# Two mixer layers: the second attention's projections placed beside the first attention's steps, groups started at fixed steps

## The reference, cut to what matters

```python
proj = x @ w_in + b_in
(qa, ka, va, beta_raw, a_raw, za, qb, kb, vb, qc, kc, vc) = jnp.split(proj, split_at, axis=-1)
o_a = gated_deltanet(qa, ka, va, beta_raw, a_raw, za, ...)   # convolution, gates, delta rule by chunks
o_b = chunk_relpos_attention(qb, kb, vb, rel_bias)           # 4 heads of 128
o_c = swa_sink_attention(qc, kc, vc, sinks)                  # 8 heads of 64, 2 of keys and values
gates = jax.nn.sigmoid(x @ w_gate + b_gate).reshape(b, t, 3, d)
merged = (gates[:, :, 0] * (o_a @ w_br_a) + gates[:, :, 1] * (o_b @ w_br_b)
          + gates[:, :, 2] * (o_c @ w_br_c))
return merged @ w_out
```

## Time and profile before

| | |
|---|---|
| median of 3 runs | 2259.19 us (2258.14 to 2260.42) |
| span of the profiled execution | 2258.2 us |
| instructions in it | 34613 |
| TensorE busy | 2223.4 us, 98% |
| VectorE busy | 1630.9 us, 72% |
| ScalarE busy | 1198.2 us, 53% |
| POOL busy | 129.2 us, 6% |
| read from HBM | 403.98 MB, mean 180 GB/s |

### The profile page before, as it was taken

One profiled execution on the slowest core, in us unless ns is written; L12 is line 12 of the kernel. 1 busy time (PEld: TensorE's weight loads), 2 busy tenths in 40 slices (PEclk: granted clock), 3 DMA queues, 4 the chain that ended last, 5 costly groups with the idle time before them and its releaser, 6 DMA issues.

```text
span 2258.2 us, 34613 instructions
## 1 busy us (share of the span) xinstructions
PE 2223.4 (98%) x14127; PEld 1903.4 (84%) x14127; DVE 1630.9 (72%) x2508; ACT 1198.2 (53%) x1896; POOL 129.2 (6%) x185
## 2 busy tenths in 40 slices
PE   8999999999999999999999999999999999989999
PEld 7888899878888888888898777888878888867887
DVE  5777768867676876768668867776877678666776
ACT  5555446644555545555356444555454655546553
POOL 2100010120000000000100110000000000420000
PEclk9999999999999999999999999999999999999999
DMA  7755574445555556656554446555655655643654
GB/s 242 226 190 188 186 226 122 141 140 187 189 186 194 188 185 210 191 188 198 194 180 141 141 136 211 189 187 174 205 173 176 207 187 188 197 128 118 197 178 149
DMA packets 284207, 408.17 MB, mean 181 GB/s; under 512 B 13828, under 2 KB 171072, under 8 KB 283792
## 3 DMA queue, kind: packets, MB, share of 16 engines
q1 hardware_dynamic: 276096, 380.84, 52.6%
q0 software_dynamic: 7808, 25.04, 3.8%
q10 hardware_dynamic: 144, 0.07, 0.0%
HBM read 403.98 MB, written 1.91 MB: 180 GB/s over the span
## 4 chain that ended last, share of the span: by engine, by line
PE 89%; DVE 6%; ACT 3%; DMA 1%; issue 1%; POOL 0%; SPq 0%; DVEq 0%; ACTq 0%
PE PS L569 24%; PE PS L475 12%; PE PS L477 12%; PE PS L476 12%; PE PS L568 11%; PE PS L472 2%; PE PS L473 2%; PE PS L474 2%; PE PS L571 2%; DVE WL L1385 2%; PE PS L552 1%; PE PS L551 1%; PE PS L550 1%; PE PS L492 1%; DVE QX L1692 1%
## 5 line engine op out<-in xcount | busy, mean ns | idle before, releaser
L1385 DVE TENSOR_TENSOR WL<-RW,WH 128x1024 fp32r<-128x1024 f32 (+2 forms) x678 | 805.6, 1222 | 168.6 <-ACT WH L1001 164.5
L569 PE MATMUL PS<-XT,WH 128*128 128x512 f32 x2368 | 807.9, 394 | 0.0
L1001 ACT ACTIVATE WH<-RW 128x1024 fp32r<-128x1024 f32 (+2 forms) x678 | 680.9, 1042 | 210.9 <-PE PS L477 44.1
L568 PE MATMUL PS<-XT,WL 128*128 128x256 f32 x2072 | 580.7, 280 | 0.0
L569 PEld LDWEIGHTS PS<-XT,WH 128*128 128x128 f32 x2368 | 425.2, 188 | 76.0
L568 PEld LDWEIGHTS PS<-XT,WL 128*128 128x128 f32 x2072 | 389.8, 188 | 13.4
L475 PE MATMUL PS<-WH,XT 128*128 128x512 f32 (+3 forms) x624 | 241.5, 387 | 1.5 <-issue 0.7
L477 PE MATMUL PS<-WH,XT 128*128 128x512 f32 (+3 forms) x624 | 233.4, 374 | 0.0
L476 PE MATMUL PS<-WL,XT 128*128 128x512 f32 (+3 forms) x624 | 233.2, 374 | 0.0
L475 PE MATMUL PS<-WH,HTH 128*128 128x512 f32 x488 | 192.4, 394 | 0.0
L477 PE MATMUL PS<-WH,HTL 128*128 128x512 f32 x488 | 191.7, 393 | 0.0
(11 more groups left out here) (513 smaller groups left out, 3256.2 us busy)
## 6 DMA issues: line engine op xcount, KB each, us to landing
RW<-in_w_ff_in SPq DMA_DIRECT2D x252, 512.0 KB, 4.3
RW<-in_w_ff_out SPq DMA_DIRECT2D x128, 512.0 KB, 4.4
RW<-in_w_in SPq DMA_DIRECT2D x56, 512.0 KB, 4.5
RW<-in_w_gate SPq DMA_DIRECT2D x48, 512.0 KB, 4.2
RW<-in_ffn_gate SPq DMA_DIRECT2D x44, 512.0 KB, 4.4
RW<-in_ffn_up SPq DMA_DIRECT2D x44, 512.0 KB, 4.7
RW<-in_ffn_down SPq DMA_DIRECT2D x44, 512.0 KB, 4.5
RW<-in_w_out SPq DMA_DIRECT2D x16, 512.0 KB, 5.0
```

The source lines that it names most:

```text
L568: self.e.matmul(k.PS[:, b.n, 0:T], wl, k.XTH[:, kt, :], start=False, stop=False)
L569: ins = self.e.matmul(k.PS[:, b.n, :], wh, k.XT[:, kt, :], start=kt == 0, stop=kt == 7)
L1001: self.e.activation(u.hi_out, raw, ACT.Copy).then_inc(*self.s["hi"].up(u.n))
L1385: self.e.tensor_tensor(u.lo_out, raw, u.hi_out.bitcast(F), ALU.subtract).then_inc(*self.s["lo"].up(u.n))
```

## The change

The projections of attention c become the generator `inputs_c`, the first part of `inputs_a`: 8 half steps for the queries, 4 steps for keys and values. The swap of the keys is done behind the first half step of the first of delta's projections. The filler then has 44 steps. The nine groups start at the steps 0, 4, 8, 14, 18, 22, 26, 30 and 34 in place of 0, 3, 6 ... 24, so that `attend` has 44 steps too.

```diff
         while gens or live:
-            if gens and n % 3 == 0:
-                live.append(gens.pop(0))
+            while gens and n >= gens[0][0]:
+                live.append(gens.pop(0)[1])
...
-        bks = [self.bank() for _ in range(4)]
-        run(self.cols(w_in, 3592, 4, bks, self.x))
-        for j in range(4):
-            e.query_c(l, j, bks[j])
-            self.drop(bks[j], ("proj_v", (l, "qc", j)))
-        kb, vbs = self.bank(), [self.bank(), self.bank()]
-        for k0 in range(0, 8, KU):
-            u = self.take(wsrc(w_in, k0, KU, 4104, 256))
-            e.kv_part(u, k0, kb, vbs, self.x)
-            self.free(u)
-        e.kv_out(l, kb, vbs)
...
-        b = self.bank()
-        e.kv_swap(l, b)
-        self.drop(b, ("proj_v", (l, "kc2")))
...
+        def inputs_c():
+            bks = [self.bank() for _ in range(4)]
+            yield from self.cols(w_in, 3592, 4, bks, self.x, steps=2)
+            for j in range(4):
+                e.query_c(l, j, bks[j])
+                self.drop(bks[j], ("proj_v", (l, "qc", j)))
+            kb, vbs = self.bank(), [self.bank(), self.bank()]
+            for k0 in range(0, 8, KU):
+                u = self.take(wsrc(w_in, k0, KU, 4104, 256))
+                e.kv_part(u, k0, kb, vbs, self.x)
+                self.free(u)
+                if k0 == 6:
+                    e.kv_out(l, kb, vbs)
+                    self.drop(kb, ("proj_v", (l, "kc")))
+                    for t in range(2):
+                        self.drop(vbs[t], ("proj_v", (l, "vc", t)))
+                yield
+
+        def swapped():
+            b = self.bank()
+            e.kv_swap(l, b)
+            self.drop(b, ("proj_v", (l, "kc2")))
+
         def inputs_a():
+            yield from inputs_c()
             for part in (0, 1, None, 2):
...
                 bks = [self.bank() for _ in range(4)]
-                yield from self.cols(w_in, 512 * part, 4, bks, self.x, steps=2)
+                yield from ending(self.cols(w_in, 512 * part, 4, bks, self.x, steps=2), 0 if part == 0 else None, swapped)
...
-        self.attend(gens, fill)
+        self.attend(list(zip((0, 4, 8, 14, 18, 22, 26, 30, 34), gens)), fill)
```

More of the change, by code:

```diff
@@ L2934, in mixer1 @@
                 self.drop(bks[j], ("proj_v", (l, "qk", 4 * part + j)))
-        bks = [self.bank() for _ in range(4)]
-        run(self.cols(w_in, 3592, 4, bks, self.x))
-        for j in range(4):
-            e.query_c(l, j, bks[j])
-            self.drop(bks[j], ("proj_v", (l, "qc", j)))
-        kb, vbs = self.bank(), [self.bank(), self.bank()]
-        for k0 in range(0, 8, KU):
-            u = self.take(wsrc(w_in, k0, KU, 4104, 256))
-            e.kv_part(u, k0, kb, vbs, self.x)
-            self.free(u)
-        e.kv_out(l, kb, vbs)
-        self.drop(kb, ("proj_v", (l, "kc")))
-        for t in range(2):
-            self.drop(vbs[t], ("proj_v", (l, "vc", t)))
-        b = self.bank()
-        e.kv_swap(l, b)
-        self.drop(b, ("proj_v", (l, "kc2")))
         todo = []
```

## The result

The changed kernel takes 2280.82 us, the median of four runs (2279.79 to 2286.09). The kernel before, in four runs beside it, takes 2258.66 us (2256.7 to 2260.42). The ratio is 1.0101, with an interval of 1.0084 to 1.0118: slower by 22.2 us. The forecast was 2258.4 us, with a range of 2253 to 2264, so the result lies outside it, on the side that had a chance of 0.14. The profiled execution of the changed kernel took 2286.09 us, the longest of the four, with a span of 2284.3 us.

What follows compares the result with a forecast made beforehand. TensorE, with work 98% of the span and 89% of the chain, was taken to bound the kernel. Terms -4.2 + 1.9 + 0.2 + 3.2 + 1.7 - 3.6 = -0.8 us off 2259.2 gave about 2258.4 us, range 2253 to 2264.

Steps and rivals of the forecast that it cites:

- the side that had a chance of 0.14: Whole kernel: slower by over 0.2%, chance 0.14.
- Part 1: Attention stretch, both layers: three TensorE waits for PSUM banks and small ones beside them go, -4.2 us.
- the waits only move within the attention stretch: Rival, attention stretch: other bank pairs come close, half the bank gain, -2.1 us; total 2260.5 us; chance 0.2.
- Part 2: First group's scores in the first attention: they come too early for their key and query sums, +1.9 us.
- Part 3: Attention stretch: possible new waits, mainly a tight bank for the second projection's fourth column, +0.2 us.
- Part 4: Ahead of the delta rule: five gate steps run instead of six, shifting the gate rhythm, +1.3 us.
- The flip: L703, delta rule: TensorE arrives one step sooner, VectorE 0.5 us sooner, so the wait grows, +1.7 us.
- The levels: Delta rule levels 1 and 4: less TensorE work covers the gate chain, waits about double, +3.2 us.
- The state step: L764, delta rule: weight cuts no longer stand ahead of the state sum, -3.6 us with some return at L1808.
- The clock: TensorE's granted clock: full in both stretches, no forecast wait long against present ones, so nothing counted.
- One step missing ahead of the delta rule decides: Slower rival: flip and both levels each lose 1.37 us, state wait only moves, +6.1 us, 2265 us; chance 0.15.
- The faster case: Rival: attention and state waits go, shift costs little at levels and flip, -5.2 us, 2254 us; chance 0.25.

Runs made afterwards that it cites:

- e4: Changed kernel with first two groups at steps 2 and 5, and follow-up items added only after the last eviction, giving six gate steps before the delta rule; 2259.20 us.
- e1: Changed kernel with the six follow-up items added only when the projections are done, so six gate steps again run ahead of the delta rule; 2263.44 us.
- e2: Kernel before, with the first of six follow-up items popped at once without a gate step, leaving five ahead of the delta rule; 2276.78 us.
- e5: Kernel before, with the last two follow-up items popped together: five gate steps, first activation still behind the first weight cuts; 2266.49 us.
- e6: Kernel before, with the first follow-up item popped at once and one filler step added behind the six items, keeping six gate steps; 2268.88 us.
- e9: e4 with the second attention's six groups on every third step from 14 instead of every fourth; 2257.14 us.
- e10: e4 with no follow-up item popped on the step of the z sums, so that item and all behind it come later; 2256.47 us.
- e7: e4 with one more filler step, seven gate steps in all ahead of the delta rule; 2258.07 us.
- e11: e9 with one more filler step, seven gate steps ahead of the delta rule; 2255.35 us.

## Why the prediction was wrong

**Part 1, the waits in the attention stretch (-4.2 us): wrong in the sum.** The three bank waits of L615, L472 and L475 went, as forecast. Two others came: 1.0 us at L637 and 0.5 us at L646, in both layers, as much as had gone. The rival "the waits only move within the attention stretch" had the mechanism, with half of the gain left; nothing was left. In e4, with the two losses mended, the mixers are 0.5 us longer each by starts, where 2.1 us shorter each was forecast. VectorE's timeline in the changed kernel shows the first:

```profile
394.81 0.15 DVE L1581 TENSOR_TENSOR SX<-PS,GB 128x8 f32<-128x8 f32 x1
394.88 1.51 DVE L1692 SCALAR_TENSOR_TENSOR QX<-QP,VEC,QX 128x256 f32<-128x256 f32 x3
396.31 0.15 DVE L1619 TENSOR_TENSOR SX<-SX 128x2 f32<-128x2 f32 x1
...
396.70 0.69 DVE L1625 TENSOR_TENSOR PP<-PP,SX 128x512 f32<-128x512 f32 x1
```

Before, the z sums stood behind a softmax end and a bank came free late. Now the last group's softmax end stands behind the z sums and three taps, and its transposes are late. I had looked only at whether a softmax stood ahead of the z sums, and not at what stood behind them.

**Part 2, the first scores (+1.9 us): right in place, too small.** 3.6 us in the two layers (2.1 and 1.5), and the clock fell behind the first (1.1 to 1.5 us more, by the estimate above). The upper end was 2.6. That a weight cut stands ahead of the sums was in the forecast; that its weights can land late was not. ScalarE's timeline in the changed kernel:

```profile
312.13 1.06 ACT L1001 ACTIVATE WH<-RW 128x1024 fp32r<-128x1024 f32 x1 [1.36 <-DMA RW<-in_w_in]
```

VectorE's cut then comes at 313.22 and the sums only at 314.37, 0.7 us behind the start of the last projection matmul (313.70). Before they stood at 311.98, 0.8 us ahead of that matmul, as the next one starts at 312.85. (The whole execution is 1 us later at this point, so the slip is 1.4 us and not the 2.4 between the two times.) It differs from run to run: in e1, with the same group starts, the weights of the same cut are there at 310.13, and the waits are 1.5 and 1.0 us. e1 and e4 price the part, with waits of 2.5 us and no fall of the clock, at 4.2 us by the medians and 3.0 by starts.

**Part 3, new waits inside the stretch (+0.2 us).** None of those that I had looked at appeared. The swap of the keys costs nothing.

**Part 4, one step lost ahead of the delta rule (+1.3 us): the step that failed.** That the change loses this step was right, and e2 shows that it is the cause of 19.0 us, most of the loss, though the forecast gave it almost nothing. Term by term, for the two layers:

- *The flip, forecast +1.7 us, measured +6.0 in waits (0.3 to 3.3 us, twice).* The failing sentence is "VectorE does too, in part: its taps are no longer queued behind a weight cut, which I put at 0.5 us". The sign was wrong. I saw that the taps move ahead of a cut and not that the activation with its table load of 1.28 us moves ahead of it as well, on ScalarE, from which VectorE's cut waits. VectorE came 3.3 us later instead of 0.5 sooner. TensorE's 1.37 us sooner was right (e5: 1.4). The upper end was 2.7 us.
- *The first product behind the convolutions, L681, forecast nothing, measured +3.0.* A wait of 1.5 us per layer for L1129, 3.0 us in all, with no term in the sum. It comes from the same queue: L1129 stands behind the last activation and its two cuts. e5, which keeps the order, hasn't got it; e6, which has six steps, hasn't either. It needs both parts.
- *The levels, forecast +3.2 us, measured +0.8 (0.6 to 0.8 us, four times).* The chain has the length of the earlier trace rows, 5.1 us from the start of L1864 at 452.13 to the end of L1153 at 457.21. But I let it start where the gate step ends, which is where L714 starts, at 452.81. VectorE's first addition takes the bank of the first half and starts 0.7 us ahead of that. 5.1 - 0.7 = 4.4 us against a cover of 3.5 leaves about the 0.8 that is seen.
- *The state step, forecast -3.6 us, measured +2.6.* L764 fell from 1.8 to 0.4 us, as forecast. Two pairs of cuts that had stood ahead of L1821 then stood ahead of L1808. L784 waits 0.8 us behind the first, a pair of plain length (2.36 us, at 507.03), and L792 waits 1.9 us behind the second, the long one. I had put 0.3 us a layer for that.

For the long pair VectorE's timeline in the changed kernel:

```profile
515.96 0.69 DVE L1821 TENSOR_TENSOR SS<-PS,gSSD 128x512 f32<-128x512 f32 x1
...
517.76 4.16 DVE L1385 TENSOR_TENSOR WL<-RW,WH 128x1024 fp32r<-128x1024 f32 x2
521.95 0.69 DVE L1808 SCALAR_TENSOR_TENSOR VN<-PS,gUU 64x512 f32<-64x512 f32 x1
```

with POOL's beside it:

```profile
517.33 3.51 POOL L2236 TENSOR_TENSOR MG<-MG,GT 128x512 f32<-128x512 f32 x2 [12.02 <-DVE GT L1872]
```

and what TensorE pays:

```profile
522.69 1.09 PE L792 MATMUL PS<-VN,gAT 64*64 64x128 f32 x16 [1.93 <-DVE VN L1808]
```

The two cuts take 4.16 us beside two additions of POOL, where such a pair takes 2.36 us alone. The long pair moved with its POOL additions, from in front of one value that TensorE needs to in front of the next. The trace agrees here with the Trainium skill (SBUF — State Buffer, "Practical consequences"), whose rule the prediction had beside its sum, and with which the term came to -0.6 us; the wait was still larger than that.

The waits of part 4 add up to 6.0 + 3.0 + 0.8 + 2.6 = 12.4 us, as the views above have it (9.7 - 3.5, twice), against +1.3 forecast.

**The clock, forecast nothing.** I wrote that no forecast wait was long against those already there. The waits that came were longer than forecast, and 13.6 us in the mixers ran at 1.2 GHz. The place is shown by the windows. The price is an estimate, 4.4 to 6.0 us: it goes by the layers of e2 and e6, which have equal waits and differ by 3.4 us at 1.2 GHz (e2 262.8 and 263.9 us from L475 to L492, e6 261.3 and 259.8 us).

**The rivals.** "One step missing ahead of the delta rule decides" named the right mechanism and came out on the right side, with 6.1 us for it and a chance of 0.15. It let TensorE's side of the loss decide, one step of 1.37 us at each place, and did not have the queue order on ScalarE. That its side came out is not to its credit: its sum is 6 us for 22. The faster case is out; where its two conditions are given (e4), there is no gain.

**What stays open.** e1 lies 5.6 us over the kernel before by the medians, and the waits in its trace explain 2.7 of them (5.5 - 2.8). By starts its two mixers lose 2.2 and 1.7 us, 3.9 in all. The trace can't show the rest: the profiled execution took 2260.79 us, 2.7 us under e1's median, and its span is only 0.8 us over that of the kernel before, so the two differ outside the mixers too, where nothing was changed. Nor is it known why e9 is 1.2 us shorter than e4 up to L659 in the first mixer, while its waits there are only 0.5 us less.

## What to carry to other kernels

When a loop of filler steps comes to end exactly where its work ends, look at what the pass behind it does: an item that loses its filler step moves ahead of whatever that step had put into the queues, and each queue must be read anew for it, the producer's queue first. Here a table load and an activation ahead of a cut cost VectorE two idle microseconds twice over, and with them all that was queued behind the cuts. A removed wait for a bank or a sum is worth nothing until what stands behind it in the same queue has been looked at: the three bank waits, the wait of L764 and the wait of L637 in e10 each came back at another instruction, with more than half of their size.

Where medians can't tell two kernels apart, the time between two fixed instructions in the traces may: here the two layers of the kernel before, of e4, e7, e9, e10 and e11 agree within 0.12 us, and from kernel to kernel a mixer differs by up to 1.8 us.

## What the runs showed of the hardware

A granted clock that falls was not expected in a kernel whose TensorE is busy 98% of the span. The kernel before has it too, outside the mixers: 0.59 from 1992 to 2000 us, in the second block. And it isn't told by the length of a wait. Behind 2.1 us (L624) and 3.3 us (L703) in the changed kernel it fell, and behind the 1.5 us of L624 in e1 it didn't. But waits of one length went both ways, from the shortest to the longest. In e2 TensorE waits 3.32 us at L703 of the first layer, as long as in the changed kernel, and has the full clock behind it (the wait ends at 430.09):

```profile
430.00:436.00 6.00, 5.91 (x85) 5.28 (x86) 5.93 (x9) 3.09 (x4) 1.31 (x1) 1.00 0.35 132
```

At L764 the kernel before waits 1.75 us and has the full clock behind it, and e6 waits 1.74 us and has 0.58 from 512 to 516 us. At L792 the changed kernel waits 1.93 us and has the full clock before and behind (the wait ends at 522.69):

```profile
517.00:522.00 5.00, 3.76 (x28) 2.73 (x24) 4.97 (x5) 0.00 (x0) 3.51 (x2) 1.00 0.19 57
522.70:528.00 5.30, 5.30 (x37) 4.44 (x38) 2.35 (x7) 2.49 (x11) 0.00 (x0) 1.00 0.31 99
```

e5 waits 1.92 us at the same L792 (until 513.09), with the full clock from 505 to 513 us, and TensorE then ran near 1.2 GHz:

```profile
514.40:517.80 3.40, 3.40 (x11) 2.80 (x10) 1.62 (x5) 1.89 (x10) 0.00 (x0) 0.54 0.27 102
```

So a wait of some 2 to 3 us in these kernels costs its own length, or that and 1.1 to 1.5 us more for a stretch of 3.4 us (about twice that for the stretches of 6.8 us, an estimate). That such a stretch may come belongs into the bounds of a forecast.

The wait at the first scores also differs from one execution to the next with the arrival of a weight tile: 2.1 and 1.5 us in the first layer of the changed kernel and of e1, with the same group starts. Such a place can't be costed from one trace to better than about half a microsecond.
